# A token's first expert row written plainly with its residual in it, the second added in memory, and gathered rows stored without the norm weight

## What is computed

```python
n = rms_norm(x, norm_ffn)                   # x / sqrt(mean(x*x) + eps) * gain
g_sel = argmax(softmax(n @ w_group))        # one of 4 groups
top_v, top_i = top_k(logits_of_group, 2)    # 2 of its 8 experts
gate = p_group * softmax(top_v)
y = x + sum over the two experts e of gate_e * ((silu(n @ w_gate[e]) * (n @ w_up[e])) @ w_down[e])
```

## Time and profile before

| | us |
|---|---|
| median of 3 runs (lowest, highest) | 1089.93 (1089.51, 1091.01) |
| the profiled execution's own time | 1091.88 |
| its span, first to last instruction | 1090.1 |
| busy in the span: PE, weight load, DVE | 1045.2, 826.0, 544.4 |
| busy in the span: ACT, POOL | 309.3, 174.6 |

### The profile page before, as it was taken

How to read it: one execution, slowest core, us unless ns; L and a number is a source line. 1 busy time by engine, 2 the same in 40 slices (tenths; PEclk the granted TensorE clock), 3 DMA queues, 4 the chain that set the end, 5 groups by cost and what they waited for, 6 DMA issues and landing times.

```text
span 1090.1 us, 29226 instructions
## 1 busy us (share of the span) xinstructions
PE 1045.2 (96%) x12774; PEld 826.0 (76%) x12774; DVE 544.4 (50%) x1052; ACT 309.3 (28%) x592; POOL 174.6 (16%) x160
## 2 busy tenths in 40 slices
PE   8999999999999999999999999999999988898996
PEld 7999999966666549899876898756898556565665
DVE  5327654378875543444734544555455534343431
ACT  6323332266775552222411011101110111101011
POOL 1001200599200000100010111111111111111102
PEclk9999999999999999999989999999999999999999
DMA  7356785000116467767899999999999999999994
GB/s 244 109 166 211 217 272 155 1 13 2 40 31 211 146 232 251 245 220 277 312 351 393 379 383 385 386 383 375 386 379 382 379 390 388 392 390 389 390 389 111
DMA packets 85816, 293.19 MB, mean 269 GB/s; under 512 B 13425, under 2 KB 44849, under 8 KB 60069
## 3 DMA queue, kind: packets, MB, share of 16 engines
q1 hardware_dynamic: 78277, 273.30, 67.2%
q0 software_dynamic: 7280, 17.58, 6.8%
q10 hardware_dynamic: 128, 0.39, 0.1%
HBM read 272.98 MB, written 42.87 MB: 290 GB/s over the span
## 4 chain that ended last, share of the span: by engine, by line
PE 73%; DMA 18%; DVE 4%; SPq 2%; ACT 1%; issue 1%; POOL 0%; ACTq 0%; POOLq 0%
PE bank L2827 20%; DMA w_all<-in_w_up 18%; PE bank L2375 12%; PE bank L2612 8%; PE bank L2418 4%; PE bank L2844 4%; PE bank L2584 3%; PE bank L2547 3%; PE bank L2848 3%; PE bank L2456 3%; SPq L1042 2%; PE bank L2852 2%; DVE keep L1887 1%; PE bank L2693 1%; PE bank L2479 1%
## 5 line engine op out<-in xcount | busy, mean ns | idle before, releaser
L2827 PE MATMUL bank<-w_all,xeT 128*32 128x256 f32 x6144 | 345.6, 382 | 22.2 <-DMA w_all<-in_w_up 19.2
L2827 PEld LDWEIGHTS bank<-w_all,xeT 128*32 128x32 f32 x6144 | 254.4, 111 | 107.0 <-issue 27.9
L2202 DVE STREAM_TRANSPOSE xeT<-xg 32x256 f32<-32x256 f32 x360 | 156.5, 435 | 97.0 <-DMA xg<-n_scr,tab 91.8
L2844 PE MATMUL bank<-w_all,hT 128*32 128x256 f32 x744 | 165.6, 379 | 0.0
L2848 PE MATMUL bank<-w_all,hT 128*32 128x512 f32 x744 | 129.3, 592 | 0.0
L1887 DVE TENSOR_TENSOR_SCAN keep<-keep,unseen 128x1024 f32<-128x1024 f32 (+7 forms) x64 | 94.8, 1514 | 37.8 <-ACT keep L1439 37.7
L2375 PE MATMUL bank<-w_hi,xh 128*128 128x256 f32 x376 | 108.1, 287 | 0.0
L2375 PE MATMUL bank<-w_hi,xl 128*128 128x256 f32 x376 | 105.5, 281 | 0.0
L2375 PE MATMUL bank<-w_lo,xh 128*128 128x256 f32 x376 | 105.5, 280 | 0.0
L2844 PEld LDWEIGHTS bank<-w_all,hT 128*32 128x32 f32 x744 | 81.8, 110 | 30.3
L1681 ACT ACTIVATE sgl<-bank 128x384 f32<-128x384 f32 x32 | 15.7, 490 | 304.2 <-PE bank L2827 304.2
(11 more groups left out here) (307 smaller groups left out, 1505.9 us busy)
## 6 DMA issues: line engine op xcount, KB each, us to landing
w_all<-in_w_down SPq DMA_DIRECT2D x64, 1024.0 KB, 30.2
w_all<-in_w_gate SPq DMA_DIRECT2D x64, 1024.0 KB, 32.6
w_all<-in_w_up SPq DMA_DIRECT2D x64, 1024.0 KB, 8.9
k_scr<-in_cache_k SPq DMA_DIRECT2D x32, 256.0 KB, 3.3
v_scr<-in_cache_v SPq DMA_DIRECT2D x32, 256.0 KB, 3.5
pgk<-k_scr SPq DMA_DIRECT2D x32, 256.0 KB, 3.9
w_raw<-in_w_in SPq DMA_DIRECT2D x7, 1024.0 KB, 7.1
pgv<-v_scr SPq DMA_DIRECT2D x4, 1024.0 KB, 6.6
```

What stands on the lines that cost most here:

```text
L2202: last = dve.transpose(xeT[i][rows_of(s), :, rows_of(g)], lane[:, :, s, :])
L2827: lasts = [pe.matmul(pair_ps(i)[rows_of(q), g, :, :], xeT[i][:, k, rows_of(g)], pair_of(b, i, k, q), start=(k == 0 and g != 1), stop=(k == ...
L2844: return pe.matmul(y_right_ps(g), hT[:, ft, rows_of(g)], w[ft // 2][:, ft % 2, DA:D], start=first and g != 1, stop=ends, skip_group_check= ...
```

## The change

Three things are changed together.

1. The norm weight is no longer in the stored rows: `norm_scale` writes `xmid` divided by the root alone, `gain_last` and POOL's part of it are gone, and the weight (a column per channel group, `gain_p`) is multiplied in after the transposes, by ACT in eight products per block (`gains`), or in `block_left` and `block_right` for blocks 0 and 1. The load of the broadcast weight (`gffn`, 512 KB) becomes one of 4 KB. The root of every token is kept in `sig`.
2. A gathered row times its root is the residual. `name_residuals` and `residual_tables` make a third table, `wtab`: for every slot the root where this expert is the token's first (the lower of its two expert numbers), otherwise 0. ACT's `keep_rows(b)` writes gathered row times `wtab` to `yo` ahead of the products; DVE's `add_rows(b)` adds the down product times the gate, all 1024 columns in five instructions, where `left_rows` (ACT) and `right_rows` (DVE) wrote them. `left_rows` and `right_rows` stay for overflow blocks alone.
3. `scatter(b)` issues two indirect DMAs of 96 rows: one plain, by `tab_first` (rows that aren't the token's first are out of bounds and skipped), one that adds, by `tab_later` (first rows skipped). `result_tables` (DVE) makes these. The order of experts changes so that within each group the numbers rise (23 comes last). `store_residual` stays.

The waits and the order of POOL change: `gather(b)` also waits for `s_ya` at b-1, that is for `keep_rows(b-2)`, which reads the same buffer; it is issued behind `moved`, four blocks ahead. `keep_rows(b)` waits until both scatters of block b-2 have landed. The rest of the diff (semaphore counts, places of tables in SBUF, overflow blocks) is left out here; this is its core.

```diff
-    expert_of = list(range(NE))
-    expert_of[NE - 1 - EPG], expert_of[NE - 1] = NE - 1, NE - 1 - EPG
+    expert_of = [e for e in range(NE) if e != NE - 1 - EPG] + [NE - 1 - EPG]
...
     def scatters(b):
-        return 16 * (b + 1) if type(b) is int and b < NE - 1 else 16 * (b + 2)
+        return 32 * (b + 1) if type(b) is int and b < NE else 16 * (b + NE + 1)
     def copies(b):
-        return scatters(b) // 16 if type(b) is int else b + 2
+        return b + 1 if type(b) is int and b < NE - 1 else b + 2
...
-            sp.dma_start(gffn[:, :], norm_ffn.to_broadcast([P, D])).then_inc(s_wr, 16)
+            sp.dma_start(gain_p[:, :], norm_ffn.rearrange("a (p kt) -> p (a kt)", kt=KT)).then_inc(s_wr, 16)
...
             def gather(b):
                 pool.wait_ge(s_ix, 1 if b < NE else b - NE + 2)
                 if b >= 2:
                     pool.wait_ge(s_xt if b < 4 else s_xc, b - 1)
+                if 2 <= b < NE:
+                    pool.wait_ge(s_ya, b - 1)
                 pool.indirect_dma_start(out=xg[i][0:CAP, :], out_offset=None, in_=n_scr,
-                                        in_offset=bass.IndirectOffsetOnAxis(ap=rows_named(b, gidx), axis=0),
+                                        in_offset=bass.IndirectOffsetOnAxis(ap=column(tab, b) if b < NE else gidx[b % 2][:, 0:1].bitcast(U32), axis=0),
             def scatter(b):
...
                 pool.wait_ge(s_yd, copies(b))
                 if b >= NE:
                     pool.wait_ge(s_sx2, b - NE + 1)
+                else:
+                    pool.indirect_dma_start(out=y_all,
+                                            out_offset=bass.IndirectOffsetOnAxis(ap=column(tab_first, b), axis=0),
+                                            in_=yo[b % 2][:, :], in_offset=None,
+                                            bounds_check=T - 1, oob_is_err=False).then_inc(s_sc, 16)
                 pool.indirect_dma_start(out=y_all,
-                                        out_offset=bass.IndirectOffsetOnAxis(ap=rows_named(b, sidx), axis=0),
+                                        out_offset=bass.IndirectOffsetOnAxis(
+                                            ap=column(tab_later, b) if b < NE else sidx[b % 2][:, 0:1].bitcast(U32), axis=0),
                                         in_=yo[b % 2][:, :], in_offset=None, compute_op=ALU.add,
...
-            gather(2)
+            for b in range(2, 4):
+                gather(b)
             pool.wait_ge(s_yst, 16 * LAST)
             pool.wait_ge(s_yl, 16)
             pool.wait_ge(s_ln, 2)
             for b in range(NE - 1):
-                if b + 3 < NE:
-                    gather(b + 3)
                 scatter(b)
                 if b < NE - 2:
                     moved(b)
+                if b + 4 < NE:
+                    gather(b + 4)
...
-                act.activation(xeT[i][:, 0:KT // 2, :], xT_ps[:, 0:KT // 2, 0:CAP], ACT.Copy).then_inc(s_xe, 1)
+                for k in range(KT // 2):
+                    last = act.activation(xeT[i][:, k, :], xT_ps[:, k, 0:CAP], ACT.Copy, scale=gain_p[:, k:k + 1])
+                last.then_inc(s_xe, 1)
+            def gains(b, i):
+                act.wait_ge(s_xc, b + 1)
+                for k in range(KT):
+                    last = act.activation(xeT[i][:, k, :], xeT[i][:, k, :], ACT.Copy, scale=gain_p[:, k:k + 1])
+                last.then_inc(s_xe, 1)
+            def keep_rows(b, i):
+                act.wait_ge(s_gl[i], 16 * (b // 2 + 1))
+                if b < 2:
+                    act.wait_ge(s_tab, 1)
+                else:
+                    act.wait_ge(s_sc, scatters(b - 2))
+                act.activation(yo[i][:, :].rearrange("r (p k) -> r p k", p=P), xg[i][0:CAP, :].rearrange("r (k p) -> r p k", p=P),
+                               ACT.Copy, scale=wtab[:, expert_of[b]:expert_of[b] + 1]).then_inc(s_ya, 1)
...
             def first_act():
                 for b in range(2):
                     block_left(b, b)
+                for b in range(2):
+                    keep_rows(b, b)
                 silu(0, 0)
+                gains(2, 0)
             def block_act(i, b):
                 silu(b + 1, 1 - i)
-                left_rows(b, i)
+                if b + 3 < NE:
+                    gains(b + 3, 1 - i)
+                if b + 2 < NE - 1:
+                    keep_rows(b + 2, i)
             def last_act(b):
                 if b == NE - 2:
                     silu(b + 1, 1)
-                    left_rows(b, 0)
...
+            def name_residuals(q):
+                lo, hi = BATCHES[q]
+                ts, n = slice(lo, hi), hi - lo
+                if q == 2:
+                    dve.wait_ge(s_tbp, 2)
+                places = tmp32[:, 0:n, 0:2 * EPG].rearrange("p t (k e) -> p k t e", k=2)
+                numbers = io_row[:, 0:EPG].rearrange("p (x y e) -> p x y e", x=1, y=1).to_broadcast([P, 2, n, EPG])
+                chain.link(dve.tensor_tensor(places, oh[:, :, ts, :], numbers, ALU.mult))
+                chain.link(dve.reduce_sum(turn[:, :, ts], places, axis=AXX))
+                for k in range(2):
+                    chain.done(dve.tensor_tensor(weight[:, k, ts], turn[:, k, ts], turn[:, 1 - k, ts], ALU.is_lt))
+                chain.settle()
+                chain.link(dve.tensor_tensor(weight[:, :, ts], weight[:, :, ts],
+                                             sig[:, ts].rearrange("p (x t) -> p x t", x=1).to_broadcast([P, 2, n]), ALU.mult))
+                return dve.tensor_tensor(residual_table(q), ek[:, :, 0:n, :], each(weight[:, :, ts], NE), ALU.mult)
...
-                rows = [a.rearrange("r (p k) -> r p k", p=P) for a in (xmid[0:r, t, :], gffn[0:r, :])]
-                dve.scalar_tensor_tensor(out=xg[t % 2][0:r, :].rearrange("r (k p) -> r p k", p=P), in0=rows[0],
-                                         scalar=rs[0:r, c], in1=rows[1], op0=ALU.mult, op1=ALU.mult).then_inc(s_n2, 1)
+                dve.tensor_scalar(xg[t % 2][0:r, :].rearrange("r (k p) -> r p k", p=P),
+                                  xmid[0:r, t, :].rearrange("r (p k) -> r p k", p=P), rs[0:r, c], None, ALU.mult).then_inc(s_n2, 1)
...
-            dve.wait_ge(s_gn, 2)
-            dve.wait_ge(s_tbp, 4)
-            chain.link(dve.tensor_copy(gtab[:, 0:NE], tab_ps[:, NE:2 * NE]))
+            name_residuals(2).then_inc(s_gn, 1)
+            dve.wait_ge(s_gn, 3)
+            def result_tables():
+                dve.wait_ge(s_tbp, 5)
+                chain.done(dve.tensor_copy(gtab[:, 0:NE], tab_ps[:, NE:2 * NE]))
+                chain.link(dve.tensor_copy(wtab[:, :], tab_ps[:, 2 * NE:3 * NE]))
+                chain.done(dve.tensor_scalar(tab_first[:, :], wtab[:, :], 0.0, float(2 * T), ALU.is_equal, ALU.mult))
+                chain.done(dve.tensor_scalar(tab_later[:, :], wtab[:, :], 0.0, float(2 * T), ALU.is_gt, ALU.mult))
+                chain.settle()
+                for names in (tab_first, tab_later):
+                    chain.done(dve.tensor_tensor(names[:, :], names[:, :], tab[:, 0:NE], ALU.add))
...
             def block_right(b, i):
                 dve.wait_ge(s_xt, blocks_turned(b))
                 since(dve, s_gp, 8 * b - 8)
-                dve.tensor_copy(xeT[i][:, KT // 2:KT, :], xT_ps[:, KT // 2:KT, 0:CAP]).then_inc(s_xc, 1)
+                gain = gain_p[:, KT // 2:KT].rearrange("p (k x) -> p k x", x=1).to_broadcast([P, KT // 2, CAP])
+                dve.tensor_tensor(xeT[i][:, KT // 2:KT, :], xT_ps[:, KT // 2:KT, 0:CAP], gain, ALU.mult).then_inc(s_xc, 1)
...
             def turn_rows(b, i):
                 dve.wait_ge(s_gl[i], 16 * (b // 2 + 1))
                 dve.wait_ge(s_gp, 8 * b - 8)
-                dve.wait_ge(s_xe, b)
                 for g in range(LANES):
                     lane = xg[i][rows_of(g), :].rearrange("r (k s c) -> r k s c", k=KT, s=QUARTERS)
                     for s in range(QUARTERS):
                         last = dve.transpose(xeT[i][rows_of(s), :, rows_of(g)], lane[:, :, s, :])
-                    if g == LANES - 2:
-                        last.then_inc(s_xe, 1)
...
+            def add_rows(b, i):
+                dve.wait_ge(s_dp, 8 * b + 8)
+                dve.wait_ge(s_ya, b + 1)
+                gates = gates_of(b, i)
+                def add(rows, cols, product):
+                    out = yo[i][rows, cols]
+                    return dve.scalar_tensor_tensor(out=out, in0=product, scalar=gates[rows, :], in1=out, op0=ALU.mult, op1=ALU.add)
+                add(slice(0, CAP), slice(0, 512), y_left_ps)
+                add(slice(0, CAP), slice(512, DA), y_mid_ps)
+                for g in range(LANES):
+                    last = add(rows_of(g), slice(DA, D), y_right_ps(g))
+                last.then_inc(s_yd, 1)
...
                     block_right(b, b)
+                result_tables()
                 count_overflow()
                 hidden(0, 0)
                 turn_hidden(0)
...
             def block_dve(i, b):
                 hidden(b + 1, 1 - i)
```

(20 more changed lines are left out.)

68 lines of the change are left out of this document (31 added, 37 removed).

## The result

| | before | after |
|---|---|---|
| median (lowest, highest), us | 1090.47 (1089.51, 1093.62), 4 runs | 1142.47 (1140.44, 1144.42), 4 runs |
| profiled execution's own time, span | 1091.88, 1090.1 | 1144.42, 1142.5 |

The ratio is 1.0471, 95% interval 1.044 to 1.0503: slower by 52 us. The forecast was 1143, 53 more.

The account below looks back on a forecast made before the run. PE, then weight transfers bound the expert blocks; after the change a 19.4 us loop, floor 17.4, taken as 18.4. Start 623.1, 24 blocks 441.6, last three 46.6, end 32.0 give 1143.3, forecast 1143 us, range 1116 to 1172.

Parts of the forecast that it names:

- What bounds now and what takes its place: Expert blocks: PE sets 15.54 us a block, later weight transfers 17.6; after the change a closed loop through the gather binds.
- The loop's length: Per block: keep_rows 1.15, hand-over 0.8, gather 9.2, transposes 5.4, gains 2.8, sum 19.4 us; 18.4 taken after relief.
- half relieved: Gathers partly shortened by gaps in DMA, putting the pace midway between unrelieved 19.4 us and DMA's floor of 17.4.
- The gains: ScalarE, per block: eight products of 128x96 at about 0.35 us each, 2.8 us, between 1.0 and 2.9.
- The middle: Pace of 24 blocks taken as 18.4 us, midway between the unrelieved loop's 19.4 and DMA's floor of 17.4.
- The start: Up to block 4: router stage 2.4 us and result_tables 1.2 later, then keep_rows(2) waiting for block 0's scatters to land.
- G(2): G(b) is the start of block b's gate and up product on TensorE; G(2) was forecast at 587.5 us, G(4) at 623.1.
- The end: Behind block 31's start: 29.2 us, plus 0.8 for add_rows and 2.0 for one more DMA on POOL, 32.0.
- Removed transfer time: DMA in the stage: 1072 plain first rows save 8.0 us, skipped rows cost 2.0, net 6.0.
- Floor: Rival: gaps shorten gathers or gains cost near 1.0, so blocks run at DMA's 17.4 us; about 1119 us, chance 0.17.
- the second loop: keep_rows, silu, hidden, add_rows, hand-over, second scatter issue, landing, keep_rows: 17.4 us a block, hidden while the first is longer.
- Faster: Rival: the loop hides and transfer savings count in full; 1087 us, needing 5.9 us from gather issue to transposes; chance 0.04.

Follow-up runs that it names:

- e1: Changed kernel, keep_rows reading a constant table of the same size instead of the gathered rows, so the gather no longer waits for it: 1116.99 us.
- e12: Changed kernel with a third buffer for result rows alone, in place of one half slot of the weights' ring: 1142.72 us.
- e11: Changed kernel with third buffers for gathered and result rows, one half slot fewer, gather(b+4) issued ahead of scatter(b): 1089.16 us.
- e2: Changed kernel with keep_rows reading the gathered row in its stored order, residual channels left unpermuted: 1138.44 us.
- e8: e6 with the first scatter adding too, all else equal: 1093.82 us.
- e6: Changed kernel's two scatters and tables, but left_rows and right_rows in place of keep_rows, gains and add_rows; gather waits for transposes alone: 1086.26 us.
- e3: Changed kernel with gains as one VectorE product behind the transposes instead of eight on ScalarE: 1128.96 us.
- e5: Changed kernel with gains as one VectorE product, as in e3, and ScalarE doing keep_rows(b+1) behind silu(b+1) in place of keep_rows(b+2): 1115.88 us.

## Why the prediction was right, point by point

- **What bounds now and what takes its place: right.** "keep_rows(b+2), which is queued behind gains(b+3)", gather and transposes form a closed loop that PE waits for. e1 (one wait), e12 (the other buffer alone) and e11 (both buffers, with POOL's gather moved ahead) show it from three sides.
- **The loop's length: 18.4 forecast, 18.44 measured**, from gains(4), which ends at 614.23, to gains(28) at 1056.81, 24 turns. ScalarE's timeline after:

```profile
581.59 2.23 ACT L1701 ACTIVATE xeT<-xeT,gain_p 128x96 f32<-128x96 f32 x8 [11.10 <-DVE xeT L2259]
...
612.00 2.23 ACT L1701 ACTIVATE xeT<-xeT,gain_p 128x96 f32<-128x96 f32 x8 [13.90 <-DVE xeT L2259]
...
1054.58 2.23 ACT L1701 ACTIVATE xeT<-xeT,gain_p 128x96 f32<-128x96 f32 x8 [14.32 <-DVE xeT L2259]
...
1100.20 2.23 ACT L1701 ACTIVATE xeT<-xeT,gain_p 128x96 f32<-128x96 f32 x8 [9.78 <-DVE xeT L2259]
1102.34 2.13 ACT L1711 ACTIVATE yo<-xg,wtab 96x1024 f32<-96x1024 f32 x1
...
1116.60 0.49 ACT L1718 ACTIVATE sgl<-bank 128x384 f32<-128x384 f32 x1 [11.75 <-PE bank L2911]
```

  Its terms were less good than their sum. Over blocks 5 to 28: keep_rows 2.14 (1.15 forecast), hand-over 0.9 (0.8), gather 7.7 (9.2 loaded, about 8.2 half relieved), transposes 5.4, gains 2.2 (2.8). One term was 1.0 too short and two together 1.1 too long, so an agreement to 0.04 is luck. keep_rows was taken from a row that reads in order, with the scattered read as a bound; the row of VectorE for scattered access was the nearer one. The Trainium skill (SBUF — State Buffer, Door 1), which says that each new 16-byte line pays a penalty, spoke against the change rightly: e2's 1.13 against 2.14 agrees, and the unrelieved addition is 1.0 us, not 0.8.
- **The gains: 2.8 was too much.** Eight ACTIVATEs of 361 ns each overlap and take 2.23 together, 0.27 apart. The Trainium skill (ScalarE: Activation LUTs, Rules for kernel authors) would have made it 3.0; the row decides against both.
- **"The middle" between 17.4 and 19.4 was a choice, and the mechanism behind it holds**: gathers are 1.2 us shorter than before, DMA's share from 600 to 1040 us fell from 1.02 to 1.00. The give-back is somewhat more than half: e2 took 1.0 us out of the loop and the pace fell by 0.36.
- **The start: gains(2) end at 583.8 and gains(4) at 614.2, where G(2) and G(4) were 587.5 and 623.1.** Ahead of G(2), the 2.4 us for the router stage and the 1.2 for result_tables weren't there: the count of overflows ends at 564.4, against 568.1 forecast and 564.5 before. The step that failed most is the way from G(2) to G(4), 30.4 us and not 35.6. The forecast had keep_rows(2) wait for the landing of block 0's scatters. There the second scatter follows the first after 1.25 us, not 2.0, because a plain one holds POOL for 0.94 us and not 1.4; and the scatters of block 0, issued to 589.81, had landed before keep_rows(2) began at 595.60, within 5.8 us where I had put 9.7. What keep_rows(2) stood behind was gains(3), without a pause. The scatters met an emptier DMA (a share of 0.93 from 580 to 600 us, 1.01 before), as the earlier trace rows could have told.
- **The end: 40.1 us behind gains(31), not 32.0.** PE starts block 31 at 1105.5, 3.0 us after its gains, and its product takes 11.1 us, not 10.4. The 2.8 for add_rows and one more DMA on POOL came to 1.9: the last half scatter is issued at 1130.29, 13.7 behind the last silu, where it was 11.75. Some 5 us more lie between that issue and the end, 12.2 against 7.0 before. The last packet lands 3.3 to 3.4 us behind the issue in both, then the trace has no work until the end; this stretch is 3.7 to 8.8 us long from kernel to kernel, and its cause stays open.
- **The last three blocks: 15.2 each by their gains, 15.54 forecast.** TensorE starts them 16.2 apart. It had waited 2.8 us for gains(28), and then its product for block 28 took 12.6 us at a granted clock of 0.86, a price that the forecast didn't have.
- **The sum**: -8.9 at the start, +1.0 in the middle, -1.0 in the last three, +8.1 at the end: 1142.5 against a span of 1143.3. By TensorE's starts, as G was defined, it is -6.4, -1.5, +2.0 and +5.1. Either way, errors of some 7 to 10 us on both sides cancelled, and that part is luck; the pace, which carries 442 of the 559 us behind G(2), didn't need that.
- **Removed transfer time: 8.0 forecast for plain writes, 7.6 measured** (e8 less e6); net 6.0 less up to 2.8 given back, 4.2 measured.
- **The rivals.** "Floor", 1119, is what one gets with the first loop cut (1117) or both rearranged (1116). I had given the second loop 17.4 with 2.0 for the second issue and 9.7 for the landing; it was the next to bind, at 17.9 in e3. In "Faster" a slip: with the end of 32.0 that the sum uses, G(31) must come at 1055, not 1058, so 16.0 a turn. That changes nothing here.

## What to carry to other kernels

When an added step reads a buffer that a later transfer refills, write out the closed loop: every instruction from the buffer's release to its next, over all engines and over what is queued ahead of each on its own. Then count by how many blocks one turn of the loop advances, and divide by that. It isn't simply the number of buffers: here the rows have two buffers, but keep_rows(b+2) is queued behind gains(b+3), so one turn advances one block, and the whole 18.4 us count. In e5, where that queueing is gone, it is two blocks a turn. Compare with the pace of the busiest engine, not with that of the transfers, for a loop between the two leaves the lead unused that prefetched data gives. Here 4.4 us of ScalarE work in a loop through two buffers cost 52 us, and the same 4.4 us with three buffers, and the gather issued earlier, cost next to nothing; adding only the buffer of the loop that doesn't bind gave nothing.

## What the runs showed of the hardware

- ScalarE, a product of 96x1024: 2.14 us with a read of four-byte elements 512 bytes apart, 1.13 in order.
- Small ACTIVATEs overlap: 361 ns each, 0.27 us apart for 96 columns.
- An indirect DMA that writes plainly holds POOL for 0.94 us, one that adds 1.45; issued back to back, the second starts 1.25 and 1.74 us behind the first.
- 1072 rows of 4 KB written plainly in place of adding save 7.6 us of a transfer-bound stage (e8 less e6).
- Gathers of 96 rows, from issue to the transposes: 8.9 us on average before, with DMA's share at 1.02, and 7.7 in the changed kernel, at 1.00.
- TensorE's clock fell to its lower level after waits for the gains: a gate and up product of 10.6 us at full clock took 12.6.
